# A two-block transformer kernel: the final norm moved into the experts' stage, low parts at set pauses, softmax in pairs of heads

## The reference, cut to what matters

```python
# gated delta rule, per head and chunk of 64
a = where(strict, einsum('id,jd->ij', kb, k) * decay, 0.0)
t_inv = triangular_solve(a + eye, eye)            # unit lower triangle
u = t_inv @ (v * beta);  w = t_inv @ (kb * exp(gc))
# experts, per token: 8 heads, 16 of 128 keys twice, 16 of 256 pairs
top_v, top_i = top_k(sc, 16)
best_v, best_pos = top_k(cand, 16)
act = gelu(u_table[expert] . x);  out = sum(gate * act * v_table[expert])
x = rmsnorm(x + out, norm_final_w)                # end of the first block
# attention, per head: compressed (15 keys), selected and window (256 keys)
p = softmax(q k^T + bias) for each; o = g0*p_c v_c + g1*p_s v_s + g2*p_w v_w
```

## Time and profile before

| what | value |
|---|---|
| median of three runs | 2430.88 us (2430.63 to 2431.09) |
| the profiled execution | 2430.28 us; its span, first to last instruction, 2428.5 us |
| busy of the span | PE 93%, DVE 64%, ACT 46%, POOL 3% |
| mean granted clock of PE | 0.960 |
| HBM read | 382.83 MB |

### The profile page before, as it was taken

How to read it: one execution, slowest core, us unless ns; L and a number is a source line. 1 busy time by engine, 2 the same in 40 slices (tenths; PEclk the granted TensorE clock), 3 DMA queues, 4 the chain that set the end, 5 groups by cost and what they waited for, 6 DMA issues and landing times. The chain is left out here.

```text
span 2428.5 us, 38500 instructions
## 1 busy us (share of the span) xinstructions
PE 2268.4 (93%) x15466; PEld 2084.1 (86%) x15466; DVE 1552.0 (64%) x2829; ACT 1128.0 (46%) x1966; POOL 75.0 (3%) x36
## 2 busy tenths in 40 slices
PE   8978788899999999999998999999999999878998
PEld 8867676899999998888888998979998899856998
DVE  7857445799888995666655456665456554494554
ACT  5523334345555445555554444444443444384443
POOL 0121000410000000000000000000000000000000
PEclk9989889999999999999998999999999999888999
DMA  6362233345444445666646555535555555303552
GB/s 261 135 69 88 90 124 136 108 156 174 151 146 147 148 149 173 192 195 194 192 138 234 190 182 218 191 128 219 190 178 194 224 187 191 115 12 122 191 190 105
DMA packets 78312, 390.27 MB, mean 161 GB/s; under 512 B 9772, under 2 KB 12716, under 8 KB 49741
## 3 DMA queue, kind: packets, MB, share of 16 engines
q1 hardware_dynamic: 76684, 383.59, 45.9%
q0 software_dynamic: 1040, 4.19, 1.6%
q10 hardware_dynamic: 432, 0.33, 0.0%
HBM read 382.83 MB, written 5.24 MB: 160 GB/s over the span
## 5 line engine op out<-in xcount | busy, mean ns | idle before, releaser
L246 DVE TENSOR_TENSOR split_slots<-ring,split_slots 128x1024 fp32r<-128x1024 f32 x396 | 470.9, 1234 | 331.5 <-ACT split_slots L237 331.5
L339 PE MATMUL banks<-x_transposed_hi,split_slots 128*128 128x256 f32 x1920 | 548.5, 286 | 9.3 <-DVE split_slots L246 5.2
L340 PE MATMUL banks<-x_transposed_lo,split_slots 128*128 128x256 f32 x1920 | 546.9, 285 | 0.0
L341 PE MATMUL banks<-x_transposed_hi,split_slots 128*128 128x256 f32 x1920 | 546.8, 285 | 0.0
L237 ACT ACTIVATE split_slots<-ring 128x1024 fp32r<-128x1024 f32 x406 | 404.3, 1049 | 222.6 <-PE banks L341 196.9
L350 DVE SCALAR_TENSOR_TENSOR expert_lo<-ring,expert_hi 128x512 fp32r<-128x512 f32 x512 | 360.3, 708 | 190.5 <-ACT expert_hi L345 189.7
L345 ACT ACTIVATE expert_hi<-ring 128x512 fp32r<-128x512 f32 x512 | 323.2, 632 | 276.4 <-PE banks L341 276.4
L339 PEld LDWEIGHTS banks<-x_transposed_hi,split_slots 128*128 128x128 f32 x1920 | 371.4, 193 | 11.9 <-DVE split_slots L246 5.6
L340 PEld LDWEIGHTS banks<-x_transposed_lo,split_slots 128*128 128x128 f32 x1920 | 371.3, 193 | 1.5
L341 PEld LDWEIGHTS banks<-x_transposed_hi,split_slots 128*128 128x128 f32 x1920 | 371.2, 193 | 0.0
L339 PE MATMUL banks<-x_transposed_hi,expert_hi 128*128 128x256 f32 x1024 | 296.8, 290 | 17.6 <-DVE expert_lo L350 17.2
(11 more groups left out here) (465 smaller groups left out, 3489.3 us busy)
## 6 DMA issues: line engine op xcount, KB each, us to landing
ring<-in_ffn_w SPq DMA_DIRECT2D x132, 1024.0 KB, 4.8
ring<-in_peer_u SPq DMA_DIRECT2D x128, 512.0 KB, 3.5
ring<-in_peer_v SPq DMA_DIRECT2D x128, 512.0 KB, 4.2
ring<-in_w_in SPq DMA_DIRECT2D x16, 1024.0 KB, 5.5
ring<-in_sgu_w_in SPq DMA_DIRECT2D x16, 1024.0 KB, 4.8
ring<-in_peer_wq SPq DMA_DIRECT2D x8, 1024.0 KB, 5.0
ring<-in_sgu_w_out SPq DMA_DIRECT2D x8, 1024.0 KB, 4.8
ring<-in_kv_w SPq DMA_DIRECT2D x6, 1024.0 KB, 5.0
```

Source lines behind the costliest of these rows:

```text
L246: ins = dve.tensor_tensor(self.parts[:, b, 1, p], self.k.w.slot(g)[:, p], self.parts[:, b, 0, p].bitcast(F32), ALU.subtract)
L339: pe.matmul(out, lh, rh, start=start, stop=False)
L340: pe.matmul(out, lh, rl, start=False, stop=False)
L341: return pe.matmul(out, ll, rh, start=False, stop=stop)
```

## The change

It has six parts. The strict triangle is masked in the exponent instead of by a multiplication, and POOL's last four products in `gdn_prepare` wait for the second set of transposes. In the experts' stage the low parts of weight slots 3 to 7 move from POOL to DVE: slot 3 before head 0, the others at pauses that a table sets; the first two expert blocks' high parts come behind heads 4 and 5; head 2 fills only from its eleventh pause; `DEPTH` goes from 42 to 47, so that each head makes 18 low parts and not 16. The last two v blocks go row tile by row tile. The gain and the next stage's three slots are asked for in this stage, and `RmsNorm` runs at its end, with `Beginning` ahead of it; `final_norm` is gone. Its squares and gain lie in blocks 48 to 59 of the expert weights, and the split slots keep their place into the second block. `attend` goes by pairs of heads: one instruction of DVE for two heads, buffers by pair, and `scores`, `turn`, `mix`, `turn` on PE. In `attend` the number of ACT's and PE's instructions is as before.

```diff
-    c[:, C_STRICT] = same & (i > j)
+    c[:, C_STRICT] = np.where(same & (i > j), 0, NEG)
...
-            link(dve.scalar_tensor_tensor(low[:, :, :], up[:, :, :], -1.0, over_middle(s.mask(C_NEG_LOW), PAIRS),
+            link(dve.scalar_tensor_tensor(low[:, :, :], up[:, :, :], -1.0, over_middle(s.mask(C_STRICT), PAIRS),
...
-            link(dve.tensor_tensor(A[:, :, :], A[:, :, :], over_middle(s.mask(C_STRICT), PAIRS), ALU.mult))
...
+            pool.wait_ge(squared, 2)
             pool.wait_ge(vs, 7)
             pool.tensor_tensor(kbg[:, :, :], kn, over_last(col[:, 1, :], P), ALU.mult).then_inc(pools, 1)
...
-DEPTH = 42
+DEPTH = 47
 FILL_FROM = 2
+SLOT_LOWS = {(0, 1): 4, (1, 0): 5, (1, 7): 6, (1, 14): 7}
...
             for n in range(2 * KEYS):
                 tiles.load(sp, n)
+            sp.wait_ge(w_low, SPARE_BLOCKS + 12)
+            sp.dma_start(gain, k.a["norm_final_w"].partition_broadcast(P)).then_inc(gain_landed, 16)
+            k.w.hold = 1 << 30
+            for n in range(RING):
+                sp.wait_ge(tiles.low_done, 2 * tiles.last_in_slot(n) + 2)
+                k.w.issue(sp, g0 + PEER_HEADS + n + 1)
...
-            for m in range(KEYS):
+            for m in range(KEYS - 2):
                 v_products(m)
+            for i in range(TILES):
+                for m in (KEYS - 2, KEYS - 1):
+                    ins = last_v_products(m, i)
+                ins.then_inc(norm.tile_done, 1)
+            norm.tensor(pe)
...
-                if h >= PEER_HEADS - 2:
+                if h in (4, 5):
                     for half in range(2):
-                        tiles.high(act, h - PEER_HEADS + 2, half)
+                        tiles.high(act, h - 4, half)
...
+            norm.scalar(act)
...
-            for m in (3, 4):
-                split.low(pool, m)
...
-                if h == 0:
-                    for m in (5, 6, 7):
-                        split.low(pool, m)
...
-            for m in range(3):
+            for m in range(4):
                 split.low(dve, m)
...
-                head(h, lambda: fill(most))
+                pauses = [0]
+
+                def between():
+
+                    slot = SLOT_LOWS.get((h, pauses[0]))
+                    pauses[0] += 1
+                    if slot is not None:
+                        split.low(dve, slot)
+                    elif h > FILL_FROM or pauses[0] > 10:
+                        fill(most)
+                head(h, between)
...
-            dve.wait_ge(tiles.eaten, 4 * KEYS)
-            for t in range(TILES):
-                dve.tensor_tensor(k.x[:, t, :], accumulated(k, t), k.x[:, t, :], ALU.add).then_inc(added, 1)
-
-
-def final_norm(k):
...
+            norm.vector(dve)
...
+        if self.begin and self.begin_first:
+            self.begin.lows(dve)
         add(0)
         dve.wait_ge(*self.gain_landed)
         scale(0)
...
+        if self.begin and self.begin_first:
+            self.begin.highs(act)
         act.activation(self.warm[:, :], k.eps[:, 0:1], ACT.Sqrt)
         squares(0)
...
-            for n in range(NH + 3):
-                if n < NH and n % 2 == 0:
-                    scores(pe, n // 2)
-                if 2 <= n < NH + 2:
-                    turn(pe, n - 2)
-                if n >= 4 and n % 2 == 0:
-                    mix(pe, (n - 4) // 2)
...
+            for n in range(NH // 2 + 3):
+                if n < NH // 2:
+                    scores(pe, n)
+                if 2 <= n < NH // 2 + 2:
+                    turn(pe, 2 * (n - 2))
+                if n >= 3:
+                    mix(pe, n - 3)
+                if 2 <= n < NH // 2 + 2:
+                    turn(pe, 2 * (n - 2) + 1)
...
-            dve.tensor_tensor(second[b][:, :, :], both(k.psum[:, bank, :], B), over_middle(s.bias[:, h, 0:B], 2),
-                              ALU.add).then_inc(biased, 1)
...
+            dve.tensor_tensor(second[b][:, :, :, :], both(0, B), near(0, B), ALU.add).then_inc(biased, 1)
...
-            for n in range(NH + 2):
-                if n >= 2:
-                    copy(n - 2)
-                if n < NH:
+            for n in range(NH // 2 + 3):
+                if 2 <= n < NH // 2 + 2:
+                    copy(2 * (n - 2))
+                    copy(2 * (n - 2) + 1)
+                if n < NH // 2:
                     exps(n)
-                if n >= 5 and n % 2 == 1:
-                    output((n - 5) // 2)
-            output(NH // 2 - 1)
+                if n >= 3:
+                    output(n - 3)
```

More of the change, by code:

```diff
@@ L1948, in halves, with last_in_slot @@
         return self.hi[:, n % 2, own], self.lo[:, n % 2, own]
+    def last_in_slot(self, s):
+        return max(n for n in range(2 * KEYS) if n % 6 // 2 == s)
     def load(self, sp, n):
@@ L2612, in vector @@
             self.low(dve, b)
-        if self.begin:
+        if self.begin and not self.begin_first:
             self.begin.lows(dve)
@@ L2649, in out_and_rms_norm @@
         split = Splitter(k, ctx, g0)
-        norm = RmsNorm(k, ctx, split, gain, gain_landed, slots, begin)
+        norm = RmsNorm(k, ctx, gain, gain_landed, begin)
         @block.sync
@@ L3431, in head, with spread, mask @@
-        def head(dve, h, last):
+            for n in range(NH // 2 + 3):
[7 more added lines that the diff above has]
+                    turn(pe, 2 * (n - 2) + 1)
+        def spread(ap, n):
+            return ap.unsqueeze(3).broadcast_to([P, 2, 2, n])
+        def mask(dve, q):
+            own = cs[q % 3][:, :, :, 0:NCMP]
+            dve.wait_ge(expd, q + 1)
+            dve.tensor_tensor(own, own, masks[:, :, 0:NCMP].unsqueeze(1).broadcast_to([P, 2, TILES, NCMP]), ALU.mult).then_inc(vs, 1)
@@ new lines, in weigh @@
+        def weigh(dve, q):
+            b = q % 3
+            dve.wait_ge(vs, 5 * q + 5)
+            own = cs[b][:, :, :, 0:NCMP]
+            dve.tensor_tensor(own, own, spread(c[b][:, 2, :, :, 0], NCMP), ALU.mult)
+            dve.tensor_tensor(first[b][:, :, :, :], first[b][:, :, :, :], spread(c[b][:, 2, :, 0, 1:3], A), ALU.mult)
+            dve.tensor_tensor(second[b][:, :, :, :], second[b][:, :, :, :], spread(c[b][:, 2, :, 1, 1:3], B), ALU.mult
+                              ).then_inc(weighed, 1)
@@ L3441, in head @@
-            dve.tensor_tensor(second[b][:, :, :], both(k.psum[:, bank, :], B), over_middle(s.bias[:, h, 0:B], 2),
-                              ALU.add).then_inc(biased, 1)
-            dve.tensor_tensor(first[b][:, :, :], both(k.psum[:, bank + 1, :], A), over_middle(s.bias[:, h, P:P + A], 2),
-                              ALU.add).then_inc(biased, 1)
-            between()
+            b, h = q % 3, 2 * q
+            dve.wait_ge(scored, q + 1)
+            if q >= 3:
+                dve.wait_ge(turned, 2 * q - 4)
@@ L3463, in _ @@
+            for _ in range(3):
+                between()
         @block.vector
@@ L3473, in _ @@
             dve.wait_ge(k.bias_spread, 16)
-            for n in range(NH + 1):
-                if n < NH:
-                    head(dve, n, n - 1 if n >= 1 else None)
+            for n in range(NH // 2 + 1):
+                if n < NH // 2:
+                    pair(dve, n, n - 1 if n >= 1 else None)
                 else:
@@ L3479, in _ @@
                         step(dve, n - 1)
-                if n >= 6 and n % 2 == 0:
-                    output((n - 6) // 2)
-            for j in range(NH // 2 - 2, NH // 2):
+                if n >= 4:
+                    output(n - 4)
+            for j in range(NH // 2 - 3, NH // 2):
                 output(j)
```

204 lines of the change are left out of this document (86 added, 118 removed).

## The result

The changed kernel takes 2407.70 us (median of 4 runs, 2405.86 to 2408.72), beside 2430.76 us (2430.55 to 2431.09) for the kernel before on the same chip: a ratio of 0.9904, 95% interval 0.9887 to 0.9921, or 23.1 us less, and the interval lies clear of 1. The profiled execution took 2408.72 us, with a span of 2406.9, so its span is 21.6 us shorter than the one before (2428.5). The forecast was 2413.7 in a range from 2405 to 2423.

What follows compares the result with a forecast made beforehand. PE, busy 93% of the span, was taken as the bound, leaving idle, half-clock and serial stretches. Gains 3.3 + 8.7 + 3.0 + 2.2 = 17.2 us off 2430.28 gave 2413.1, adjusted to 2413.7; range 2405 to 2423.

Steps and rivals of the forecast that it cites:

- Delta products: In gdn_prepare, folding the mask and making POOL's four products wait gains 3.3 us, bounds 0.5 and 7.2.
- the give-back: In gdn_prepare, loss from POOL's products beside the first levels: about 1.2 + 1.8 us, plus some 0.9 at half clock.
- Low parts: In the experts' stage, low parts moved to DVE at set pauses gain 8.7 us, bounds 5 and 12.
- the tail: In the experts' stage, PE's idle time from 605 to 640 us, 2.91 before, kept at 2.9 us.
- Norm: Between the two blocks, running the final norm inside the experts' stage gains 3.0 us, bounds 1.5 and 4.5.
- The begin in front of the addition: At the norm, the next slots' first high and low parts ahead of the first addition cost 1.6 us.
- Paired softmax: In attend, handling two heads per DVE instruction gains 2.2 us, bounds 9.4 and -3.3.
- The lower bound, -3.3: In attend, the paired softmax's worst gain, for half clock throughout: -3.3 us.
- Rival 1: In attend, DVE alone is the bound, so the gain is 17.2 + 7.2 us: 2406.5; chance 0.15.
- Rivals 2 and 4: Longer gap before head 3 and half-clock pair cycle: 2421.6, chance 0.17; norm and delta products give nothing: 2420.0, chance 0.10.
- rival 3: At the end of heads 3 to 7, PE's recurring gap becomes 4 us: price 23 us, 2436.7; chance 0.03.
- The scatter: In the experts' stage, 75 blocks instead of 80 for its 64 groups cost nothing, or 2 us without cover.

Runs made afterwards that it cites:

- highs_late: The changed kernel with the first expert high parts taken after heads 6 and 7 instead of 4 and 5: 2408.32 us, 0.9910 of the kernel before.
- begin_halves: The changed kernel with the second of the next slot's two low parts moved behind the first addition: 2407.16 us, 0.9904 of the kernel before.
- exps_between: The changed kernel with ACT's four long exponentials in attend put between its two copies: 2404.21 us, 0.9894 of the kernel before.

## Why the prediction was right, and where its steps were off

The direction and the range were right, and each of the four parts gains. Two of the four workings stand as forecast (delta products, norm); of the low parts one piece was wrong, and the paired softmax gains elsewhere than forecast. The forecast was 6.0 us too high (17.2 us of gain, 23.1 measured), and the larger part of that is one term.

- **Delta products: 3.3 forecast, 4.1 to 4.5 measured.** The first update came 7.5 us earlier (8.15 less the 0.68 by which this trace was ahead already), forecast 7.2. Three operations are stretched, as listed: pick, inverse, pick, the first two on the path. What was too large is the last piece of the give-back, "a PE that stands still meanwhile gives some 0.9 us more at half clock": the give-back to the next level's update was 3.0, not 3.9, and 2.8 of it are the two stretched operations (2.38 and 1.78 less 0.69 each).
- **Low parts: 8.7 forecast, 11.5 to 13 measured.** The mis-sized step is "the pause in the lows at each head's end stays ..., and so does the gap of 1.1": four gaps of 1.08, 4.3 us in all, are 0, and the tail, 2.9 us, is 1.25 (35 - 33.75). The gaps at the start were 1.51 + 3.68 = 5.2 where I had 3.5. So what PE loses after is 5.2 + 1.25 and about 1 of half clock, 7.5, and 20.3 - 7.5 = 12.8; to the first v product 12.6 were measured. The prediction had the numbers for it in its own text: 26 us of PE a head against 24.7 of DVE. Who works longer per head has no gap; I took the pace from PE and the gap from DVE. That the first high parts come behind heads 4 and 5 is worth nothing (`highs_late`).
- **Norm: 3.0 forecast, 3.2 measured** (3.7 by undoing it). PE restarts 10.42 us after the last v product, forecast 10.6. The begin in front of the addition costs the 1.0 us that `begin_halves` wins back; the prediction had 1.6.
- **Paired softmax: 2.2 forecast, 1.4 in the stage and 1.9 behind it.** The pair's cycle is 7.93 us, forecast 7.7, with ACT waiting 1.24 us between the copies, forecast 1: the wait was right, and `exps_between` shows that it is the bound. The pieces of the sum were not: the start, forecast at about 1, gained 5.1 in the first four pairs; the steady part lost 0.4 where 0.1 a pair was to be gained; and the 3.5 us more at the end stood nowhere. That 2.2 and 1.4 are near each other is luck. The lower bound, -3.3, has no working: the same text gets 77 us at half clock, against 77.1 before. What the sum left out besides is the next stage: I put the clock's part into the last mixes and not into the 5 us behind them. The Trainium skill, VectorE: DVE Perf Modes, The TRN2 errata, gives (N + 151) / 0.96 ns for an fp32 tensor_tensor, 1.22 us for 1,024 elements, and the rows agree for a single one (1.21, 1.22). By its fixed part alone, an estimate from the page, 15 instructions less would save 0.157 us each. Here 15 instructions less a pair took DVE's busy time from 7.74 to 6.76 us (13.51 / 2, `exps_between`), 0.065 us each. My sum for DVE, 6.3 us, was 0.5 too low.
- **Rivals and signs.** Rival 1 (DVE alone bounds attend) did not come; `exps_between` comes near it, with DVE at 99%, but ACT is at 98% there, and the pair takes 6.83 us. Rivals 2 and 4 and the slower rival 3 did not come: there is no recurring gap at all, and norm and delta gave 7.7 us together. The scatter cost nothing, as forecast: 860 to 880 us is full, with DVE at 18.48 of 20. Two signs read otherwise than meant. PE gaps of 1.1 us, 26 us apart, were to show the prediction right, and there are none. An idle PE between 860 and 920 was to show it wrong, and PE does stand still there for 3.06 us, up to 907.42; but that is the gap ahead of the first v product, which the kernel before has too (3.07 us, up to 924.10).

Left open: why the clock behind the same gap of 3.06 us is 0.50 in one profile and 1.00 in another. PE's work ahead of the gap is alike in them (it is full for the 20 us before), and no run here sets where the half stretches fall. Each kernel has one trace, so a difference of 2.7 us in the experts' column can be this and nothing else.

## What to carry to other kernels

A gap that comes back with every round of a loop is a balance, not an event: compare what each engine works per round, and if the consumer's share is the shorter, giving it more work per round can remove the gap, as 18 halves for 16 did here; whether a shorter pause would have was not run. Where DVE and GpSimd both read SBUF, count the stretch until the last GpSimd instruction ends as DVE's, and start GpSimd's work in DVE's waits for PE, one instruction per wait. An in-order engine that waits between two like steps wants other ready work between them; and of a stage's end ask which clock it hands to the next one. Before a small difference is put down to an edit, look at the granted clock behind each gap of PE.

## What the runs showed of the hardware that I had not expected

- Taking one DVE operation of 2.80 us from beside four POOL products gave DVE 1.1 us: the picks behind it grew from 6.06 to 7.77. Spread over DVE's waits the same POOL products cost DVE nothing, and took 1.90 to 2.36 us themselves instead of up to 2.80.
- The clock that a stage ends with is a gain or loss of the next: 12 or 22 matmuls in 5 us that are equally busy, 2.2 us in all.
- Behind one and the same PE gap of 3.06 us the granted clock was 0.50, 0.68 or 1.00 in the next 5 us, from kernel to kernel, which is 2.7 us between the extremes.
- With nothing changed in it, most stretches have the same length within 0.7 us from kernel to kernel, also when 4 or 10 us are cut ahead of them; whole kernels spread more, the single runs of the kernel before from 2425.0 to 2431.7 us.
